# A conditioned decoder layer in fp32: the first norm rebuilt with token-major sums, a diagonal of inverse RMS and conditioning in two column halves

## The reference

```python
cond = jax.nn.silu(c)
mod = (cond @ w_ada[l] + b_ada[l]).reshape(b_, N_SUB, 3, d)
h = modulate(rms_norm(x, norm_gains[l, 0]), mod[:, 0, 0], mod[:, 0, 1])   # h * (1 + scale) + shift
x = x + 0.5 * mod[:, 0, 2][:, None, :] * swiglu(h, ffn1_w_in[l], ffn1_w_down[l])   # D_FF = 2816
...
```

## Time and profile before

| | before |
|---|---|
| three runs, us | 1303.15, 1306.64, 1307.61 |
| median, us | 1306.64 |
| profiled execution: span, us | 1300.5 |
| TensorE matmul busy | 1233.2 us, 95% |
| VectorE, ScalarE, GpSimd busy | 599.4, 420.2, 85.2 us |
| mean granted TensorE clock | 0.965 |

### The profile page before, as it was taken

One profiled execution on the slowest core, in us unless ns is written; L12 is line 12 of the kernel. 1 busy time (PEld: TensorE's weight loads), 2 busy tenths in 40 slices (PEclk: granted clock), 3 DMA queues, 4 the chain that ended last, 5 costly groups with the idle time before them and its releaser, 6 DMA issues.

```text
span 1300.5 us, 14537 instructions
## 1 busy us (share of the span) xinstructions
PE 1233.2 (95%) x5707; PEld 1003.2 (77%) x5707; DVE 599.4 (46%) x684; ACT 420.2 (32%) x432; POOL 85.2 (7%) x121
## 2 busy tenths in 40 slices
...
DMA packets 119781, 143.28 MB, mean 110 GB/s; under 512 B 3892, under 2 KB 102336, under 8 KB 119744
## 3 DMA queue, kind: packets, MB, share of 16 engines
...
...
## 4 chain that ended last, share of the span: by engine, by line
issue 48%; PE 38%; DVE 7%; ACT 3%; DMA 2%; POOL 1%; SPq 0%; ACTq 0%; POOLq 0%; DVEq 0%
PE PS L458 10%; PE PS L459 10%; PE PS L460 10%; PE PS L598 3%; DVE ACC L1122 2%; ACT WH L784 1%; PE PS L536 1%; DMA ADA<-in_w_ada_dram 1%; PE PS L501 1%; PE PS L503 1%; PE PS L502 1%; DMA RAW<-in_w_in_mix_dram 1%; DVE W L1258 1%; DMA RAW<-in_ffn_w_in_dram 1%; PE PS L638 0%
## 5 line engine op out<-in xcount | busy, mean ns | idle before, releaser
L458 PE MATMUL PS<-HH,WH 128*128 128x512 f32 (+1 forms) x1000 | 406.8, 407 | 13.4 <-DVE HL L1088 11.3
L459 PE MATMUL PS<-HL,WH 128*128 128x512 f32 (+1 forms) x1000 | 399.1, 399 | 0.0
L460 PE MATMUL PS<-HH,WL 128*128 128x512 f32 (+1 forms) x1000 | 398.7, 399 | 0.0
L1066 DVE TENSOR_TENSOR WL<-RAW,WH 128x2048 fp32r<-128x2048 f32 (+2 forms) x99 | 220.9, 2232 | 349.0 <-ACT WH L784 349.0
L784 ACT ACTIVATE WH<-RAW 128x2048 fp32r<-128x2048 f32 (+2 forms) x99 | 184.1, 1860 | 412.2 <-PE PS L460 377.5
L458 PEld LDWEIGHTS PS<-HH,WH 128*128 128x128 f32 (+1 forms) x1000 | 190.8, 191 | 61.7 <-issue 14.9
L460 PEld LDWEIGHTS PS<-HH,WL 128*128 128x128 f32 (+1 forms) x1000 | 190.5, 191 | 45.8
L459 PEld LDWEIGHTS PS<-HL,WH 128*128 128x128 f32 (+1 forms) x1000 | 191.0, 191 | 44.0 <-issue 1.1
L458 PE MATMUL PS<-UH,WH 128*128 128x512 f32 x352 | 139.3, 396 | 0.0
L460 PE MATMUL PS<-UH,WL 128*128 128x512 f32 x352 | 138.9, 395 | 0.0
L459 PE MATMUL PS<-UL,WH 128*128 128x512 f32 x352 | 138.9, 395 | 0.0
...
## 6 DMA issues: line engine op xcount, KB each, us to landing
...
```

What stands on the lines that cost most here:

```text
L458: mm(ps, whi, ahi, start=start, stop=False)
L459: mm(ps, whi, alo, start=False, stop=False)
L460: return mm(ps, wlo, ahi, start=False, stop=stop)
L1066: V.tensor_tensor(WL[s][:, 0:size], RAW[s][:, 0:size], WH[s][:, 0:size].bitcast(F32), ALU.subtract)\
```

## The change

The first norm is computed another way:

- **Sums of squares token-major.** ScalarE squares the four XST tiles with a running sum per partition (token) into SS. VectorE forms V4, GpSimd raises it to -0.5 into R4 (moved in front of its fourth mask), and VectorE builds DIAG, four 128 x 128 diagonals of 1/RMS per token.
- **Normed transposes.** TensorE multiplies XST by DIAG, which transposes and scales in one matmul; ScalarE copies the result to TN0. The plain transposes remain for X: blocks 0 to 5 before DIAG, 6 and 7 behind. VectorE copies X blocks 0 to 2, ScalarE the rest. GpSimd's additions, `sum_squares(0)`, `rms(0)` and the table load before them go.
- **Conditioning in two column halves.** ADA0 comes as 2 x 8 transfers of 512 KB: half 0 holds the shift and scale columns of blocks 0 to 3, half 1 those of 4 to 7. A half is 8 terms on 1024 columns.
- **FFN 1's first pair by k-halves** (`first_pair`): k-blocks 0 to 3 of both units after half 0, k-blocks 4 to 7 after half 1; the RAW transfers and splits of units 0 and 1 are halved alike. The reduction of half 1 stands before the last low k-block of unit 1, that of piece 4 before k-block 5 of unit 1 as before.
- All eight small transfers are on ScalarE's queue. Semaphore counts that the first norm used to raise are added at the start; `swiglu_in` begins at pair 1.

```diff
-ADA0 = place("ADA0", [P, 2, DB, 2 * AW], 0)
+ADA0 = place("ADA0", [P, 2, DB, 2, AW], 0)
 XST = place("XST", [P, TT, D], 65536)
-ACC0 = place("ACC0", [P, 4, AW], HO + 2 * H_BYTES - 4 * AW * 4)
+ACC0 = [place("ACC0a", [P, 2 * AW], NT), place("ACC0b", [P, 2 * AW], 2 * FB * T * 4)]
+TN0 = place("TN0", [P, DB, T], HO + H_BYTES)
+DIAG = place("DIAG", [P, TT, P], 104448)
...
-    for dst, src in small[len(small) // 2:]:
-        sp.dma_start(dst, src).then_inc(small_in, 16)
...
-    for pair in range(2):
-        for j in range(DB // 2):
-            sp.dma_start(ADA0[:, pair, 2 * j:2 * j + 2, :],
-                         ada_rows[:, 2 * j:2 * j + 2, 2 * AW * pair:2 * AW * (pair + 1)])\
-                .then_inc(ada0_in[4 * pair + j], 16)
+    ada_parts = ada.rearrange("(k p) (s n) -> p k s n", p=P, s=9)
+    def load_ada0(half):
+        for k in range(DB):
+            sp.dma_start(ADA0[:, half, k, :, :], ada_parts[:, k, 0:2, AW * half:AW * (half + 1)])\
+                .then_inc(ada0_in[DB * half + k], 16)
...
     w1 = ffn1_w_in[0]
-    load(0, 0, raw(0), cols(w1, 0))
-    load(1, 1, raw(1), cols(w1, FF))
+    KH = DB // 2
+    load_ada0(0)
+    for n, col in ((0, 0), (1, FF)):
+        sp.dma_start(raw(n)[:, 0:KH, :], cols(w1, col, 0, KH)).then_inc(low_in[n], 16)
+    load_ada0(1)
+    for n, col in ((0, 0), (1, FF)):
+        sp.dma_start(raw(n)[:, KH:DB, :], cols(w1, col, KH, KH)).then_inc(raw_in[n], 16)
     load_ada(4 * DB, slice(4 * AW, 5 * AW))
...
-    nc.gpsimd.memset(S[:, :], 0.0).then_inc(sacc, 1)
-    for b in range(DB):
-        pool.wait_ge(sq_ready, b + 1)
-        pool.wait_ge(sacc, b + 1)
-        nc.gpsimd.tensor_tensor(S[:, :], S[:, :], SG[:, b % 2, :], ALU.add).then_inc(sacc, 1)
     for l, B in enumerate(LEVELS):
+        if l == 3:
+            pool.wait_ge(v_ready, 1)
+            nc.gpsimd.tensor_tensor(R4[:, :], V4[:, :], HALF4[:, :], ALU.pow).then_inc(r_ready, 1)
...
+    def transpose_x(b):
+        for t in range(TT):
+            ins = nc.tensor.transpose(PS[:, X0_BANK[b], t * P:(t + 1) * P], XST[:, t, b * P:(b + 1) * P],
+                                      IDENT[:, :])
+        ins.then_inc(xt_done, 1)
+    for b in (0, 1, 2, 3):
+        transpose_x(b)
+    pe.wait_ge(small_ready, 1)
+    for b in (4, 5):
+        transpose_x(b)
+    pe.wait_ge(dg_ready, 1)
     for b in range(DB):
+        if 1 <= b <= 3:
+            pe.wait_ge(xready, b)
         if b >= 4:
-            pe.wait_ge(xready, b - 3)
+            pe.wait_ge(tn_copied, b - 3)
         for t in range(TT):
-            ins = nc.tensor.transpose(PS[:, b % 4, t * P:(t + 1) * P], XST[:, t, b * P:(b + 1) * P], IDENT[:, :])
-        ins.then_inc(xt_done, 1)
-    sum_squares(0)
-    for piece in range(4):
-        pe.wait_ge(ada_acc, 2 * DB * (piece // 2 + 1) - 1 + piece % 2)
...
-        ins.then_inc(ada_red, 1)
+            ins = mm(PS[:, (3 + b) % 4, t * P:(t + 1) * P], XST[:, t, b * P:(b + 1) * P], DIAG[:, t, :],
+                     start=True, stop=True)
+        ins.then_inc(tn_done, 1)
+    for b, freed in ((6, 5), (7, 6)):
+        pe.wait_ge(tn_copied, freed)
+        transpose_x(b)
+    def ada0_reduce(half):
...
+                col = DB * s + 4 * half + m
+                ins = mm(PS[:, 6, col:col + 1], ACC0[half][:, AW * s + m * P:AW * s + (m + 1) * P],
+                         ONES[:, 0:1], start=True, stop=True)
+        ins.then_inc(ada_red, 2)
+    ada0_reduce(0)
...
-    def swiglu_in(base_n, which, with_ada):
-        with pe.Fori(0, NP) as i:
+    def first_pair():
+        for n in range(2):
...
+            for k in range(DB // 2):
+                if n == 1 and k == 3:
+                    ada0_reduce(1)
+                pe.wait_ge(h_lo, k + 1)
+                for m in range(2):
...
+                    three(PS[:, 2 * n + m, :], whi[:, k, w], wlo[:, k, w], HH[:, k, :], HL[:, k, :], k == 0, False)
+        for n in range(2):
...
+            for k in range(DB // 2, DB):
+                if n == 1 and k == 5:
+                    ada_reduce(5 * DB, 4)
+                pe.wait_ge(h_lo, k + 1)
+                for m in range(2):
...
+                    ins = three(PS[:, 2 * n + m, :], whi[:, k, w], wlo[:, k, w], HH[:, k, :], HL[:, k, :], False,
+                                k == DB - 1)
+            ins.then_inc(unit_done, 1)
+    def swiglu_in(base_n, which, with_ada, first=0):
+        with pe.Fori(first, NP) as i:
...
-    swiglu_in(N_F1IN, 0, True)
+    first_pair()
+    swiglu_in(N_F1IN, 0, True, first=1)
     pe.wait_ge(u_lo, NP)
     pe.wait_ge(u_hi, NP - 1)
     pe.wait_ge(silu_done, 1 + NP)
...
     act.wait_ge(lb_ready, 1)
...
-    exp_ln_tables()
+    act.wait_ge(x_in, 16 * TT)
+    for t in range(TT):
+        ins = A(TN0[:, 2 * t:2 * t + 2, :], XST[:, t, :], ACT.Square, accum_out=SS[:, t:t + 1])
+    ins.then_inc(ss_done, 1)
     for b in range(DB):
-        act.wait_ge(xt_done, b + 1)
-        A(X[:, b, :], PS[:, b % 4, :], ACT.Copy).then_inc(xready, 1)
-        square(b, b + 1, max(b, 1), X[:, b, :])
-    rms(0)
-    split_hi(0, 16)
-    split_hi(1, 16)
-    norm_blocks(0)
+        act.wait_ge(tn_done, b + 1)
+        A(TN0[:, b, :], PS[:, (3 + b) % 4, :], ACT.Copy).then_inc(tn_copied, 1)
+    def copy_x(b, done):
+        act.wait_ge(xt_done, done)
+        A(X[:, b, :], PS[:, X0_BANK[b], :], ACT.Copy).then_inc(xready, 1)
+    copy_x(6, 7)
+    copy_x(7, 8)
+    half_unit = UNIT // 2
...
+        act.wait_ge(low_in[n], 16)
+        A(WH[n][:, 0:half_unit], RAW[n][:, 0:half_unit], ACT.Copy).then_inc(low_hi, 1)
+    def first_blocks(half):
+        for b in range(4 * half, 4 * half + 4):
+            if b >= 2:
+                act.wait_ge(h_lo, b - 1)
+            a, sh = AV[:, 0, b:b + 1], MOD[:, b:b + 1]
+            if b % 4:
+                A(HFULL[:, b % 2, :], TN0[:, b, :], ACT.Identity, bias=sh, scale=a)
+            A(HH[:, b, :], TN0[:, b, :], ACT.Identity, bias=sh, scale=a).then_inc(h_hi, 1)
+    act.wait_ge(av_half, 1)
+    first_blocks(0)
+    for b in (3, 4, 5):
+        copy_x(b, b + 1)
+    for n in range(2):
+        act.wait_ge(raw_in[n], 16)
+        A(WH[n][:, half_unit:UNIT], RAW[n][:, half_unit:UNIT], ACT.Copy).then_inc(unit_hi, 1)
+    act.wait_ge(av_ready, 1)
+    first_blocks(1)
     silu_tables()
...
-            .then_inc(mod_ready, 4)
-        dve.wait_ge(mod_ready, 4)
-        scale_vector(0)
-        split_lo(0, 1)
-    normalise(0, vectors0, between=lambda: split_lo(1, 2))
+    for b in (0, 1, 2):
+        dve.wait_ge(xt_done, b + 1)
+        V.tensor_copy(X[:, b, :], PS[:, X0_BANK[b], :]).then_inc(xready, 1)
+    def ada0_term(half, k):
+        dve.wait_ge(ada0_in[DB * half + k], 16)
+        w = ADA0[:, half, k, :, :].rearrange("p s c -> p (s c)")
+        if k == 0:
+            V.tensor_scalar(ACC0[half][:, :], w, COND[:, 0:1], None, ALU.mult).then_inc(ada_acc, 2)
+        else:
+            dve.wait_ge(ada_acc, 2 * DB * half + 2 * k)
+            V.scalar_tensor_tensor(ACC0[half][:, :], w, COND[:, k:k + 1], ACC0[half][:, :], ALU.mult, ALU.add)\
+                .then_inc(ada_acc, 2)
+    def vectors0(half):
...
+        dve.wait_ge(ada_red, 2 * half + 2)
+        V.tensor_tensor(part(MOD[:, 0:2 * DB]), part(PS[:, 6, 0:2 * DB]), part(PT[:, PC_BADA:PC_BADA + 2 * DB]),
+                        ALU.add).then_inc(mod_ready, 2)
+        dve.wait_ge(mod_ready, 2 * half + 2)
...
+            .then_inc(av_ready if half else av_half, 1)
+    def first_lo(b):
+        if b % 4 == 0:
+            dve.wait_ge(av_ready if b else av_half, 1)
+            self_wait(V.tensor_scalar(HFULL[:, 0, :], TN0[:, b, :], AV[:, 0, b:b + 1], MOD[:, b:b + 1],
+                                      ALU.mult, ALU.add))
+        dve.wait_ge(h_hi, b + 1)
+        V.tensor_tensor(HL[:, b, :], HFULL[:, b % 2, :], HH[:, b, :].bitcast(F32), ALU.subtract).then_inc(h_lo, 1)
...
+        dve.wait_ge(low_hi, n + 1)
+        V.tensor_tensor(WL[n][:, 0:half_unit], RAW[n][:, 0:half_unit], WH[n][:, 0:half_unit].bitcast(F32),
+                        ALU.subtract).then_inc(low_lo, 1)
+    def high_split(n):
+        dve.wait_ge(unit_hi, n + 1)
+        V.tensor_tensor(WL[n][:, half_unit:UNIT], RAW[n][:, half_unit:UNIT],
+                        WH[n][:, half_unit:UNIT].bitcast(F32), ALU.subtract).then_inc(unit_lo, 1)
+    ada0_term(0, 0)
+    ada0_term(0, 1)
+    dve.wait_ge(ss_done, 1)
+    V.tensor_scalar(V4[:, :], SS[:, :], 1.0 / D, EPS, ALU.mult, ALU.add).then_inc(v_ready, 1)
+    ada0_term(0, 2)
+    dve.wait_ge(consts, 7)
+    dve.wait_ge(r_ready, 1)
+    for t in range(TT):
+        ins = V.tensor_scalar(DIAG[:, t, :], IDENT[:, :], R4[:, t:t + 1], None, ALU.mult)
+    ins.then_inc(dg_ready, 1)
+    for k in range(3, DB):
+        ada0_term(0, k)
+    low_split(0)
+    vectors0(0)
+    dve.wait_ge(tn_copied, DB)
+    first_lo(0)
+    first_lo(1)
+    low_split(1)
+    first_lo(2)
+    first_lo(3)
+    for k in range(DB):
+        ada0_term(1, k)
+    high_split(0)
+    vectors0(1)
+    first_lo(4)
```

(19 more changed lines are left out.)

44 lines of the change are left out of this document (32 added, 12 removed).

## The result

| | before | the change |
|---|---|---|
| median, us (13 runs each) | 1303.81 (1301.58 to 1307.61) | 1309.19 (1306.98 to 1312.55) |
| ratio | | 1.0041, interval 1.0030 to 1.0052 |
| profiled execution: span, us | 1300.5 | 1305.7 |
| TensorE, matmuls busy, us | 1233.2 | 1247.6 |
| mean granted clock | 0.965 | 0.970 |

The change costs 5.4 us. The forecast was 1304.2 us with a range to 1309.0, counted from 1306.64, the median of three runs. With 13 runs the kernel before stands at 1303.81, so the difference is the fairer comparison: -2.4 us forecast, +5.4 measured. The profiled execution took 1307.82 us, 2.1 more than its span.

What follows compares the result with a forecast made beforehand. TensorE, 95% busy, bounds the kernel; the start counts through VectorE's start of piece 4: 56.6 + 28.07 = 84.7 against 87.11, -2.4 us. 1306.64 - 2.4 = 1304.2 us, range 1299.5 to 1309.0.

Steps and rivals of the forecast that it cites:

- The step that failed: Whole kernel: the change is worth only what it moves TensorE's start of unit 3, forecast as -2.4 us.
- 87.11: Time in us, in the profile before, when TensorE's last wait for FFN 1's weights ends and unit 3 starts.
- A smaller step: FFN 1's start: TensorE reaches unit 3 by 84 us, before VectorE's 84.7, so VectorE sets unit 3.
- Squares, power, DIAG: First norm: four squares end at 16.0 us, then V4, power and four diagonals; DIAG ready at 18.7 us.
- the half term taken: First norm: the power waits 0 to 1.3 us for VectorE's conditioning term, taken as 0.6.
- Matmuls by DIAG: Normed transposes: 64 records in 9.0 us, until 27.7; then the first k-block ready at 33.8 us against 47.0.
- Half 1 and piece 4: Conditioning: half 1's eight terms take 10.0 us, until 48.1; 8.5 us more, and piece 4 starts at 56.6.
- Unit 3: FFN 1's second pair: piece 4 at 56.6 plus 28.07 us puts unit 3's start at 84.7 against 87.11.
- VectorE's tail: From the start of piece 4 to TensorE's start of unit 3, 28.07 us, in code that is untouched.
- the third rival: TensorE sets unit 3: all 18 matmuls after piece 4's wait at 1.2 GHz, unit 3 at 86.4, -0.7 us; chance 0.14.
- The slower rival: TensorE stays at 1.2 GHz from 18.7 us through the low half: +7.9 us, 1314.5 us; chance 0.09.

Runs made afterwards that it cites:

- e5: The change with SS placed behind the arena, so all operands lie as in the kernel before; 1303.05 us against 1302.74, ratio 1.0006.
- e1: The kernel before with one unused tensor, arena 32 B later; 1311.54 us against 1304.12, ratio 1.0063.
- e3: The kernel before with two unused tensors, arena 64 B later; ratio 1.0045 to the kernel before.
- e2: The change with one unused tensor beside SS, arena 64 B later than in the kernel before; ratio 1.0025 to the kernel before.
- e7: The kernel before with WH and WL 32 B and the arena 128 B later; ratio 1.0035.
- e8: The kernel before with HH and HL (also OUTT, ACC0) 32 B later, UH and UL in place; ratio 1.0054.
- e11: The kernel before with four unused tensors, only the arena 128 B up; 1281.97 us against 1302.44, ratio 0.9838.
- e16: The kernel before with WH, WL and everything behind them, the arena too, 128 B up; ratio 1.0002.
- e18: The kernel before with HH and HL (also OUTT, ACC0) 128 B up, UH and UL in place; ratio 0.9893.
- e19: The kernel before with WH, WL and small tensors behind them 128 B up, the arena in place; ratio 0.9827.
- e14: The change with three unused tensors beside SS, arena 128 B higher than in the kernel before; 1282.09 us against 1304.32, ratio 0.9827.
- e10: e5 with the RAW transfers of units 2 and 3 ahead of piece 4's third ADAW transfer; ratio 0.9981 to the kernel before.
- e12: e5 with 62 unused matmuls of ONES in TensorE's four gaps of the first pair; ratio 0.9973 to the kernel before.

## Why the prediction was wrong

**The step that failed** is in its first paragraph: "From there to the down product TensorE waits for nothing, and no later part is changed. So the whole change is worth what it moves 87.11." No later line was changed, but a later operand was. The waits view could not tell, as a slower matmul is no wait. The diff did: one new tensor in front of the arena. By e5 against the change this was worth 1.0041 - 1.0006, 3.5 thousandths or 4.6 us.

**A smaller step missed too**, in the sum itself: "With 11.2 for unit 2 it is at unit 3 by 84, inside 84.7." TensorE came to unit 3 at 86.34 us, behind VectorE, and so TensorE set the end of the start. What the start alone is worth stays open. With the operands in place (e5) it is +0.3 us by the medians, with an interval of the ratio of -0.7 to +2.2 us, which leaves out the -2.4 that was forecast; at 32 and 64 B the change is 2.9 and 2.6 us ahead of the kernel before.

1. *Squares, power, DIAG.* Right as a whole. A square took 1.04 us and its read of the accumulator, a second instruction, 0.19, most of it beside the square; all four were done at 15.4 us (16.0 taken). The power took 1.94 us against the 1.6 taken, behind VectorE's term of 1.28 that began 0.22 us before it: 1.03 and 0.91 of waiting. The term had 1.06 us left when the power began. The Trainium skill, page SBUF — State Buffer, section SBUF: two separate sides, has a lock that the later of the two engines waits for through the whole instruction; the trace agrees with that better than with the half term taken. It cost 0.3 us.
2. *Matmuls by DIAG.* 9.10 us, 9.0 worked out; first HH product at 33.81, 33.8 worked out. Some of that closeness is luck. The terms as written add up to 18.6, 30.6 and 33.6 us, not 18.7, 30.7 and 33.8. And 11 starts in 2.0 us and 5 in 0.6 are 0.18 and 0.12 us each, a rate one and a half times as high and not doubled, so those rows do not show the step from one clock level to the other. In the change TensorE was granted 0.50 from 18.9 to 22 us, 0.90 to 24 and 1.00 from there.
3. *Half 1 and piece 4.* A term lasted 1.28 us, but dependent terms started 1.42 apart where 1.32 was taken. That cost 0.7 us over the seven; half 1 had begun 0.4 us earlier than worked out. The reduction came at 48.48 us, piece 4 at 57.15, 0.5 us late.
4. *Unit 3.* VectorE's tail nearly held: WL of unit 3 was done at 85.8 us, 28.6 behind the start of piece 4 (28.07 taken). TensorE came later. Piece 4's reduction started at 66.76 us, where 65.7 was worked out: piece 4 was 0.5 us late, and the reduction followed it by 9.6 us (9.1 taken; the rows named give 9.2). From there to unit 2 it took 8.3 us, where 5.0 to 7 was taken, with 12 of the 18 matmuls at 0.43 us. This is the third rival, given 0.14 and worked out as 86.4 us and -0.7. That its 86.4 was met so closely is in part luck, as it had all 18 slow and the reduction 1.1 us earlier. TensorE was granted 0.50 behind the waits of 2.05 and 4.69 us. The Trainium skill, page TensorE: Matmul & The Clock Gate, section HAM oscillation — how this bites in real kernels, says the same of waits between groups of matmuls: the clock falls, and the next group starts slow.
5. *The rivals on the other side.* The slower rival was right in its sign for another reason. DIAG was not wholly slow (9.10 us, not 14.3), so the clock did not decide it. None of the rivals had a mechanism that acts behind the start.

How much of the small gain of 2 thousandths in e1 against the change and e3 against e2 is the start, and how much the kernel before loses there by a clock that falls behind its wait at unit 3 (e1: granted 0.59 in 90 to 94 us), was not told apart. One trace of each doesn't settle it. The nine traces with the start of the kernel before (before, e1, e3, e7, e8, e11, e16, e18, e19) have unit 3 at 87.11 to 90.45 us, with a mean of 88.5. The four with the start of the change (the change, e2, e5, e14) have it at 85.60 to 88.37, with a mean of 86.8. So the kernel before's own trace, on which the prediction stands, is the earliest of its kind. Nor is it known why three kernels with a remainder of 128 (e10, e12, e16) ran FFN 2 at 22.40 us a pair and four others at 22.31. Each pace was read from one execution, so it may be that it differs between executions of one kernel.
